# First mixer of a two-layer decoder step: all tokens per channel tile, 512-column convolution, weight matrices built on VectorE

## The reference

```python
def _conv_mixer(h, ctx, w_pw1, b_pw1, w_dw, b_dw, ln_g, ln_b, w_pw2, b_pw2):
    a = h @ w_pw1 + b_pw1                                        # (B, L, 2D)
    glu = a[..., :D_MODEL] * jax.nn.sigmoid(a[..., D_MODEL:])    # (B, L, D)
    full = jnp.concatenate([ctx.astype(glu.dtype), glu], axis=1) # (B, CONV_WIDTH-1+L, D)
    conv = lax.conv_general_dilated(
        full, w_dw[:, None, :].astype(full.dtype), window_strides=(1,), padding='VALID',
        dimension_numbers=('NWC', 'WIO', 'NWC'), feature_group_count=D_MODEL) + b_dw
    y = jax.nn.silu(_layernorm(conv, ln_g, ln_b))
    out = y @ w_pw2 + b_pw2
    return out, full[:, -(CONV_WIDTH - 1):]
...
        xp = xp + op
        xp = xp + _swiglu(_rmsnorm(xp, ffn_norm_g[i]), ffn_w_gate[i], ffn_w_up[i], ffn_w_down[i])
```

## Time and profile before

| | |
|---|---|
| three runs | 1807.9, 1812.1, 1810.9 us, median 1810.9 |
| profiled execution | 1810.1 us; span of its slowest core 1808.6 us |
| busy share of the span | TensorE 84%, VectorE 53%, ScalarE 22%, GpSimd 14% |
| granted clock of TensorE, mean | 0.92 |
| DMA | 124 MB, mean 69 GB/s |
| chain that ended last | TensorE 72%, VectorE 13%, issue 6%, ScalarE 4%, DMA 3% |

### The profile page before, as it was taken

The page is one execution under the profiler, slowest core; times in us unless marked ns, Lnnn a source line. Parts: engine busy times, 40 slices in busy tenths (PEclk is TensorE's granted clock), DMA queues, the critical chain, the costliest instruction groups (busy, mean ns, idle before and its releaser), DMA issues.

```text
span 1808.6 us, 24861 instructions; the slowest of 8 cores (1792.4 to 1808.6 us)
## 1 busy us (share of the span) xinstructions
PE 1525.7 (84%) x8314; PEld 726.9 (40%) x8314; DVE 956.1 (53%) x1328; ACT 398.2 (22%) x612; POOL 261.6 (14%) x158
## 2 busy tenths in 40 slices
PE   3777836676988999999995897797999999999973
PEld 1344414433434444444441443344444444444431
DVE  3398747375464252534349656865634252515278
ACT  3143453362220101010111322222110101010111
POOL 3185407510000000000002011001000000000011
PEclk8798978897989999999996998898999999999986
DMA  8952253364202040312124642213422121212013
GB/s 171 172 153 56 51 117 93 80 126 110 41 7 48 1 71 9 62 28 32 24 47 93 139 141 93 89 52 77 68 37 47 24 47 24 47 24 48 1 47 145
DMA packets 132303, 124.11 MB, mean 69 GB/s; under 512 B 5748, under 2 KB 119668, under 8 KB 131128
## 3 DMA queue, kind: packets, MB, share of 16 engines
q0 software_dynamic: 50800, 48.60, 18.1%
q1 hardware_dynamic: 81384, 73.93, 14.0%
HBM read 140.83 MB, written 31.98 MB: 96 GB/s over the span
## 4 chain that ended last, share of the span: by engine, by line
PE 72%; DVE 13%; issue 6%; ACT 4%; DMA 3%; POOL 1%; SPq 0%; DVEq 0%; ACTq 0%; POOLq 0%
PE ps L180 68%; DVE RSTD L285 3%; DVE HT L487 3%; PE ps L570 2%; DVE XT L886 2%; ACT CONV L612 1%; DVE YF L1217 1%; DVE CONV L601 1%; ACT L283 1%; PE ps L557 1%; DVE VB L1120 1%; POOL W L437 1%; DVE HCV L664 1%; DMA XT<-xt 1%; ACT RSTD L283 1%
## 5 line engine op out<-in xcount | busy, mean ns | idle before, releaser
L180 PE MATMUL ps<-HT,RB 128*128 128x512 bf16 x3328 | 750.2, 386 | 40.8 <-ACT RSTD L283 15.6
L180 PEld LDWEIGHTS ps<-HT,RB 128*128 128x128 bf16 x3328 | 325.7, 99 | 436.6 <-issue 70.1
L180 PE MATMUL ps<-HID,RB 128*128 128x512 bf16 (+1 forms) x1600 | 306.5, 352 | 37.8 <-DVE RSTD L285 22.7
L886 DVE TENSOR_TENSOR XT<-ps,XT 128x512 f32<-128x512 f32 (+1 forms) x480 | 270.8, 593 | 53.5 <-DVE XT L886 33.3
L180 PEld LDWEIGHTS ps<-HID,RB 128*128 128x128 bf16 x1600 | 139.0, 100 | 204.6 <-issue 65.2
L878 DVE TENSOR_TENSOR HID<-ps,SG 128x512 bf16<-128x512 f32 (+1 forms) x110 | 64.4, 597 | 250.4 <-PE ps L180 246.5
L878 DVE TENSOR_TENSOR HID<-ps,SGB 128x512 bf16<-128x512 f32 (+1 forms) x110 | 63.8, 596 | 243.9 <-PE ps L180 243.2
L180 PE MATMUL ps<-HT,RA 128*128 128x512 bf16 x752 | 175.1, 394 | 11.8 <-DVE CONV L601 11.7
L437 POOL TENSOR_TENSOR W<-IDS,WV 128x1152 bf16<-128x1152 bf16 x64 | 151.2, 2394 | 72.0 <-PE ps L570 63.4
L877 ACT ACTIVATE SGB<-ps 128x512 f32<-128x512 f32 (+1 forms) x110 | 57.4, 522 | 387.6 <-PE ps L180 386.8
L877 ACT ACTIVATE SG<-ps 128x512 f32<-128x512 f32 (+1 forms) x110 | 57.5, 522 | 380.9 <-PE ps L180 380.3
(11 more groups left out here) (126 smaller groups left out, 972.2 us busy)
## 6 DMA issues: line engine op xcount, KB each, us to landing
RB<-wsc_in SPq DMA_DIRECT2D x12, 1024.0 KB, 5.9
RB<-w_gate POOLq DMA_DIRECT2D x10, 1024.0 KB, 8.3
RB<-w_up POOLq DMA_DIRECT2D x10, 1024.0 KB, 9.9
RB<-w_down POOLq DMA_DIRECT2D x9, 1024.0 KB, 14.0
y_p<-YF SPq DMA_DIRECT2D x8, 1024.0 KB
RA<-w_pw POOLq DMA_DIRECT2D x12, 512.0 KB, 10.0
wsc_pw<-RA SPq DMA_DIRECT2D x12, 512.0 KB, 10.1
XT<-xt SPq DMA_DIRECT2D x6, 1024.0 KB, 12.5
```

What stands on the lines that cost most here:

```text
L180: fns.append(lambda o=o, l=l, r=r, i=i: nc.tensor.matmul(o, l, r, start=(i == 0), stop=(i == n - 1)))
L886: op(DVE, lambda: nc.vector.tensor_tensor(out=XT[:, m, t0:t0 + n], in0=ob[:, :n], in1=XT[:, m, t0:t0 + n], op=ALU.add), (obr,), (XTr[m][t],))
```

## The change

- x, HT and CONV are cut by token tile (`XTT`, `HTT`). Each channel tile is now projected for all 2048 tokens and the sample rows at once (`pw1_ct`), and convolved with 512 columns per matmul (`conv_ct`); there are no halves, no halo copies and no copy of the first mixer's weights in DRAM. Those are packed by the host so that a channel tile's block is contiguous.
- Each W9 is built once, 32 in all, by VectorE, five buffers. GpSimd only issues DMAs.
- The start goes token tile by token tile for the first three channel tiles. To make room, the W9 and CC buffers lie where x of token tile 2 was and GA and PR where tile 3 was, once these have been normalised. Tiles 2 and 3 of x are therefore read a second time ahead of the residual.
- Two PSUM banks hold the statistics, six rotate.
- The norm over channels comes after the last convolution, for tile 0, tile 1, then tiles 2 and 3 together. `y_move` takes half a token tile out and back, in pieces of 128 instead of 256 elements. `pw2` of tile 0 is cut in two: four input channel tiles for six outputs, then the other four.
- FFN0 begins with its 256-wide slice, woven into `pw2`, and ends with a whole one.

Its core, with lines left out:

```diff
...
-FFN0 = [(512 * s, 512) for s in range(5)] + [(2560, 256)]
+FFN0 = [(2560, 256)] + [(512 * s, 512) for s in range(5)]
...
-            i = (pstate["i"] % 8) if pstate["all"] else (1 + pstate["i"] % 7)
+            i = (pstate["i"] % 8) if pstate["all"] else (2 + pstate["i"] % 6)
...
+        W9 = [xat(f"W9_{i}", [128, NSH, 128], BF16, 32768 + 2304 * i) for i in range(NW9)]
+        CC = [xat(f"CC{i}", [128, 2, 512], BF16, 32768 + 11520 + 2048 * i) for i in range(2)]
+        GA = [xat(f"GA{i}", [128, 4, 8 + 512], BF16, 49152 + 4160 * i) for i in range(3)]
...
+        def load_w(c):
+            slot_load(RA[c % 3], w_pw1.rearrange("p (h b) n -> p h b n", h=2)[:, :, c, :])
+            return RA[c % 3].ap[:, :].rearrange("p (h k n) -> p h k n", h=2, k=8), RA[c % 3].res
...
-                op(POOL, lambda out=out, i0=i0, i1=i1: nc.gpsimd.tensor_tensor(out=out, in0=i0, in1=i1, op=ALU.mult),
-                   (IDSr, WVr), (W9r[sl],))
-
...
+        def w9_build():
...
+            w9["built"] += 1
+            sl = g % NW9
+            out = W9[sl][:].rearrange("p s (q i) -> p (s q) i", q=NPH)
+            i0 = IDS[:].unsqueeze(1).broadcast_to([128, NSH * NPH, 32])
+            i1 = WV[:, g, :].unsqueeze(2).broadcast_to([128, NSH * NPH, 32])
+            op(DVE, lambda: nc.vector.tensor_tensor(out=out, in0=i0, in1=i1, op=ALU.mult), (IDSr, WVr), (W9r[sl],))
...
+        def conv_group(g):
+            c, b = g // 4, g % 4
+            cv, cvr = bank()
+            sl = g % NW9
+            pe_multi([lambda s=s: nc.tensor.matmul(cv[:, :], W9[sl][:, s, :], GA[c % 3][:, b, 8 - s:520 - s],
+                                                   start=(s == 0), stop=(s == NSH - 1)) for s in range(NSH)],
+                     [GAr[c % 3], GAHr, W9r[sl]], (cvr,))
             conv_stats()
-            cs = CONV[:, 4 * c + 1:4 * c + 5, :]
-            op(DVE, lambda: nc.vector.tensor_copy(out=CC[:, :, 0, :], in_=cs), (CONVr[c],), (CBr,))
-            op(ACT, lambda: nc.scalar.activation(out=CC[:, :, 1, :], in_=cs, func=AF.Square),
-               (CONVr[c],), (CSQr,))
-            st_pend.append(c)
+            wr = [CONVr[t][c] for t in range(4)]
+            op(ACT, lambda: nc.scalar.activation(out=CONV[:, :, g + 1, :], in_=cv[:].rearrange("p (t u) -> p t u", t=4),
+                                                 func=AF.Identity, bias=vcol(V_PBDW, g), scale=1.0), (cvr, VECr), wr)
+            op(ACT, lambda: nc.scalar.activation(out=CC[g % 2][:, 1, :], in_=cv[:], func=AF.Square,
+                                                 bias=vcol(V_PBDW, g), scale=1.0), (cvr, VECr), (CCr[g % 2],))
+            op(DVE, lambda: nc.vector.tensor_copy(out=CC[g % 2][:, 0, :].rearrange("p (t u) -> p t u", t=4),
+                                                  in_=CONV[:, :, g + 1, :]), wr, (CCr[g % 2],))
+            st_pend.append(g)
+            w9_build()
...
+        def conv_ct(c):
+            for b in range(4):
+                conv_group(4 * c + b)
+                run(1)
...
+        def ln_act(t0, t1, k):
+            for g in range(8 * k, 8 * k + 8):
+                c = g // 4
+                wr = [CONVr[t][c] for t in range(t0, t1)]
+                if g % 4 == 0:
+                    wr += [CONVr[t][c - 1] if c else Y0r[t] for t in range(t0, t1)]
+                op(ACT, lambda g=g: nc.scalar.activation(out=YB[:, t0:t1, g, 0:128], in_=CONV[:, t0:t1, g + 1, :], func=AF.Silu,
                                                          bias=vcol(V_PLNB, g), scale=vcol(V_PLNG, g)), (VECr,), wr)
...
+        def y_move(t, hf):
+            d = ysc[2 * t + hf]
+            dr = Res()
+            rd = CONVr[t][4 * hf:4 * hf + 4] + [CONVr[t][3] if hf else Y0r[t]]
+            dma(SP, d.rearrange("p (g u) -> p g u", g=16), YB[:, t, 16 * hf:16 * hf + 16, 0:128], rd, (dr,))
             v = d.rearrange("(q j) (c b u) -> b j c q u", q=NPH, c=4, b=4)
-            dma_batch(SP, [(HTH[0][32 * b:32 * b + 32, c0:c0 + 4, :].rearrange("p c (q u) -> p c q u", q=NPH), v[b])
-                           for b in range(4)], (ymr[(h, c0)],), YR[h][c0:c0 + 4])
...
+        def pw1_ct(c):
+            for t in range(4):
+                pw1_unit(c, t)
+                run(1)
+            shuffle_out(c)
+            pw1_unit(c, 4)
+            if c + 3 < 8:
+                Wc[c + 3] = load_w(c + 3)
+            jobs.extend([lambda hf=hf: hist_job(c, hf) for hf in range(2)])
+
+        for c in range(3, 8):
+            pw1_ct(c)
...
+            conv_ct(c - 3)
+            shuffle_in(c)
+        jobs.extend([lambda: samp_new(6), lambda: samp_new(7), samp_fin, samp_ln])
+        conv_ct(5)
+        conv_ct(6)
+        run(len(jobs))
+        conv_ct(7)
+        conv_stats()
+        fM = fence([GSTr[2]])
+        for i in range(2):
...
+        conv_fin(0, 0, 128)
+        for k in range(4):
+            ln_dve(0, k)
+            ln_act(0, 1, k)
+            if k % 2 == 1:
+                y_move(0, k // 2)
+        for m in range(8):
+            pw2_unit(m, 4)
+        conv_fin(1, 128, 512)
+        for k in range(4):
+            ln_dve(1, k)
+            ln_act(1, 2, k)
+            if k % 2 == 1:
+                y_move(1, k // 2)
+        for c in range(8):
+            XTr[c][2] = Res(fence(W9r + CCr))
+            XTr[c][3] = Res(fence(GAr + [GAHr, PRr]))
+        xload(2, 1)
...
+        fC = [fence(CONVr[t] + [Y0r[t]]) for t in range(4)]
+        rb_open(0, fC[0])
+        rb_open(1, fC[0])
+        issue(2)
...
+        for m in range(6):
+            wP, rP = Pw[m // 2]
+            mc = (m % 2) * 128
+            pe_multi([lambda k=k: nc.tensor.matmul(banks0[m][0][:, :], wP[:, k, mc:mc + 128], pw2_mov(0, k),
+                                                   start=(k == 0), stop=False) for k in range(4)],
+                     YR[0][0:4] + [rP], (banks0[m][1],))
...
+                                                   start=False, stop=(k == 7)) for k in range(4, 8)],
+                     YR[0] + [rP], (banks0[m][1],))
+            pw2_res(banks0[m][0], banks0[m][1], m, 0)
+        for m in range(6, 8):
+            pw2_unit(m, 0)
+        for k in range(2):
+            for t in (2, 3):
+                ln_dve(t, k)
+            ln_act(2, 4, k)
+        y_move(2, 0)
+        y_move(3, 0)
+        norm_s1(0)
         for m in range(8):
...
+            pw2_unit(m, 1)
+        norm_s1(4)
+        for k in range(2, 4):
+            for t in (2, 3):
+                ln_dve(t, k)
+            ln_act(2, 4, k)
+        y_move(2, 1)
+        y_move(3, 1)
+        xload(3, 1)
+        fC = [fence(CONVr[t] + [Y0r[t]]) for t in range(4)]
+        rb_open(2, fence([Res(fC[0]), Res(fC[1])]))
+        rb_open(3, fC[1])
+        HID0 = at("HID0", [128, 4, TT], BF16, 33792)
+        HID0r = [[Res(fC[2]) for _ in range(NT)] for _ in range(4)]
+        f0n = FFN0[0][1] // 128
+        bg0, rg0 = next_block()
...
+        gu0 = lambda j, t: gate_up(bg0, rg0, bu0, ru0, HID0, HID0r, j, t)
+        norm_s2(0, V_FNG0)
+        norm_s1(1)
+        for j in range(f0n):
+            gu0(j, 0)
+        norm_s2(4, V_FNG0)
+        norm_rstd(1)
         for m in range(8):
-            pw2_unit(Pw[m // 2], RA[m // 2].res, m, 1)
...
+            pw2_unit(m, 2)
+            norm_app(1, V_FNG0, [m])
+        norm_s1(2)
+        for j in range(f0n):
+            gu0(j, 1)
+        norm_rstd(2)
         for m in range(8):
-            pw2_unit(Pw[m // 2], RA[m // 2].res, m, 4)
...
```

643 lines of the change are left out of this document (243 added, 400 removed).

## The result

The changed kernel takes 1833.6 us in its profiled execution (span 1832.5), against 1810.1 (span 1808.6) before; the ratio of the two kernels is 1.0129, 95% interval 1.0106 to 1.0152. I had forecast 1769.5 us and gave "slower" 8%. On the chip that ran n1_combo, n2_combo_ffn, n3_combo_pair and n4_noexch most executions, of the kernel before too, had one die (four cores) slowed, so those four runs stand without a ratio and are read by their rows and by the cores that were not slowed.

The account below looks back on a forecast made before the run. TensorE's waits and low clock in the first mixer were the target. Of 1808.6 us of span, 571.4 became 500 (119, 290, then 210 more), the wide slice added 30: 1767.2, plus 2.3 gives 1769.5 us; range 1745 to 1797.

Parts of the forecast that it names:

- Stage one: Start of the first mixer: three channel tiles projected for all tokens, x tile by x tile, ending at 119 us.
- tile 3's chain, to 100.6: Start of the first mixer: the norm chain of x tile 3 lets its matmuls start at 100.6 us.
- Stage two: Five projections (72.5 us), eight convolutions (76.4) and waits for VectorE (21.8), the last convolution matmul ending at 290 us.
- The statistics of a group wait for its cast: Convolutions: casts queue behind W and PR on VectorE; a group with a history job costs 4.05 us against TensorE's 2.38.
- the sixth 0.7: Sixth convolution: waits for VectorE add 0.7 us to its 9.5 us.
- In the seventh the norm of the sample rows: Seventh convolution: the sample's norm enters ScalarE's queue ahead of evictions, with casts behind it on VectorE, adding 8 us.
- Stage three: From the last convolution matmul to the first whole slice: norm, row exchange and VectorE's rounds, 210 us, ending at 500 us.
- 0.45 each: Convolution's norm after the last convolution: each Silu piece of 128 columns on ScalarE takes 0.45 us, eight 3.6 us.
- landing 4.6: Row exchange through DRAM: a y_move's rows land in 4.6 us at best, 6.6 in the middle.
- Rounds: End of the first mixer: gates (7 us), ONESM, root, RECIPROCAL and eight residual and HT pairs alternate through VectorE, to 210.
- Two: Rival, 18%: the row exchange is slow, each y_move in line costing 4.6 us more, 23 in all, giving 1793 us.
- three: Rival, 8%: slower than before, the exchange queue pacing the mixer's end as one serial chain, 49 us more, giving 1819 us.

Follow-up runs that it names:

- n1_combo: The changed kernel with the edits of m1_marks, m2_jobs, m3_quiet, m4_slot16 and q3_own_slot together; no ratio, six cores had 1762 to 1773 us.
- n2_combo_ffn: n1_combo with the first feed-forward slices ordered as before the change, 512 columns first and 256 last; medians of its dies 1779.9 and 1782.7 against 1769.8 us.
- n3_combo_pair: n1_combo with x tiles 0 and 1 normalised together, in Silus of 256 columns; the same kernel timed again had ratio 0.9803 to the kernel before.
- n4_noexch: The changed kernel without the exchange of rows through DRAM, so part of the computation is missing; 32 us earlier at the first whole slice, one execution.
- m4_slot16: The changed kernel, with the Silu of group 16 waiting only for its own slot, not the transfer out of groups 0 to 15; ratio 1.0081 to before.
- r2_before_signals: The kernel before the change, with every operation of ScalarE, VectorE and TensorE raising its semaphore; ratio 0.9763 to the kernel before.
- m1_marks: The changed kernel, with every operation of ScalarE, VectorE and TensorE signalling up to the first whole slice; ratio 1.0033 to the kernel before.
- q3_own_slot: The changed kernel, with a convolution's eviction no longer waiting for VectorE's cast of the group before; ratio 1.0082 to the kernel before.
- p4_w_gpsimd: The changed kernel with the 32 builds of W on GpSimd, as before the change; 1846.3 us in the one execution taken.
- m3_quiet: The changed kernel with x's second reads last in the exchange's queue and the first feed-forward weights after tile 1's rows; ratio 1.0118 to the kernel before.
- m2_jobs: The changed kernel with the history products, and four new-token sums, moved from the convolutions under the projections; ratio 1.0009 to the kernel before.

## Why the prediction was wrong

**What bounds the kernel: half right.** The slices and rates held (TensorE 345 of 347 us, 0.217 us per matmul, PR 1.15, and W 1.351, the value I took). By the Trainium skill ("Vector Engine (DVE) Microarchitecture Reference", Performance modes) two 16-bit elements go at once only where every operand's innermost step is 1 or -1; the trace agrees, with 1152 elements in 1351 ns where one operand has step 0. But I read waits by their sizes and took their releasers for needs. The earlier trace rows held one that wasn't: that for the transfer out of CONV (m4_slot16). The halo copy's in the earlier trace rows was a real need: with every operation signalling TensorE still waits for it. PE's waits in the kernel before, then in r2_before_signals (us in total, times, longest):

```profile
PE ps L570 <- ACT GA L707: 40.0, 4, 24.1
```
```profile
PE ps L572 <- ACT GA L709: 48.6, 4, 31.0
```

**Stage one, 11.4 us.** Failed step: "tile 3's chain, to 100.6", that is a unit paced by HT from the first HT on. It waited for the last of eight, and tile 2's for a GST (85.3 us). m1_marks moved these to 101.7 and 78.8 and the end to 134.3, against my 100.6, 80 and 133.5. The durations and the chain were right; that a wait ends when its operation does was assumed.

**Stage two, 20.5 us.** Failed step: "The statistics of a group wait for its cast". They waited for PR or a sum behind it, as ScalarE's evictions did. With signals alone (m1_marks) the stage takes 165.2 us instead of 177.0, so 11.8 of the 20.5 are late signals. A convolution is then 12.5 us where I had 12.0, and the first 13.4 where I had 12.6: the waits for VectorE's work, "the next four, with two each, 2.5 more", were nearly right (3.0; I had left out the sums of the new tokens, 1.36 us each, which also stand in that queue). In the changed kernel the same convolutions took 14.7 to 14.9. q3_own_slot (3 us) shows that the eviction's loop alone was not it, p4_w_gpsimd that W was better off on VectorE. Second failed step: "the sixth 0.7" and "In the seventh the norm of the sample rows" at 8. The sixth took 7.4 us more than 9.5 and the seventh 9.0, together 7.8 more than I gave them, and still 7.4 more in m1_marks. The queue of jobs reached the sample's norm at the end of the sixth (2.72 us of wait for VectorE's CB, 1.17 for its statistics), and VectorE's sums of the new tokens stood ahead of it. No run was made for this term alone. The projections, at 14.3 instead of 14.5, give about 1 back.

**Stage three, 34 us,** in three terms. *Silus*, 11 us: "0.45 each" was drawn between 64 columns (0.35) and 256 (0.67); a 128-column one takes 0.58 (9.29 for 16), 64 of them 8 us more, with a table load and the wait after it. *Landings*, 10 us ahead of tile 1: "landing 4.6" was taken from moves with nothing beside them, and I wrote that "DMA has little else there", though the change itself puts x's reads there and the first weights are free to start. m3_quiet has them at 5.7. *Rounds*, 12 us: from tile 0's HT (455.4) to the slice 110.5 us against 98; the gates run at 9.14 and 8.52 us instead of 7.0 after each wait, and the end waits 4.83 us for VectorE. That last wait is a late signal too: SCR at L960 is a clearing for layer 1, which the slice does not need, and in m1_marks it falls to 0.46 us, but there TensorE waits 5.54 us for w_up one block later. The rest of this term stays open; no run was made for it alone.

**The wide last slice** was right (30, measured 29.4), and so was the transfer out (4.5, measured 4.2). A move in 256-byte pieces therefore took 0.79 of the time of one in 512-byte pieces with twice the bytes. The Trainium skill ("DMA: Bandwidth & Descriptors", Specifications) says that below 512 bytes the engines read, modify and write. Read as I read it, as the whole cost for half the bytes (1.0), it was nearer to 0.79 than my lower end of 0.5, and it did not decide the case.

**Rivals.** Two and three named the exchange, at 23 to 49 us beyond my sum; the rows put its landings at 10 beyond it, and by n4_noexch all of the exchange is some 31. None named signals or ScalarE's Silus. The measured 1833.6 lies 14 us above even the slowest rival. The 8% for "slower" rested on one mechanism, where several ordinary ones added up: late signals 23 us in stages one and two, rounds 12, Silus 11, landings 10, the sample's norm 8. Each pushed the same way. And late signals are not why the changed kernel lost to the one before, which paid as much for them; they are why its own time was forecast too short, since my sum took the measured 571.4 us away, with its late signals, and put ideal waits in its place.

## What to carry to other kernels

Before you redesign a stage, look at who *releases* each wait and whether the waiter needs it; where the named operation is a later one on that engine, let the needed one signal first (43 us here from two added lines, without any redesign). Look where a queue of small jobs really puts each of them: moved under a stretch in which their engine is idle, they cost nothing (m2_jobs). When a transfer is moved or taken out of a cover, list everything that the same change lets start beside it.

## What the runs showed of the hardware

- VectorE, ScalarE and TensorE raising a semaphore with every operation (TensorE with the last matmul of a group) cost nothing that can be seen: four whole slices take 345.8 us in r2_before_signals, 347.8 without.
- The pace of short ScalarE work may depend on whether each waits for the one before. In the changed kernel the 128-column Silus of CONV, which do, last 493 ns and follow every 580; the 64-column ones of the sample, which don't, last 426 ns and follow every 345:

```profile
L597 ACT ACTIVATE CONV<-CONV,VEC 128x128 bf16<-128x128 f32 x64 | 31.5, 493 | 14.4 <-DMA ysc<-CONV 8.7
L671 ACT ACTIVATE HT<-HCV,VEC 128x64 bf16<-128x64 f32 x8 | 2.8, 426 | 0.0
```

  That would be why a value drawn between 64 and 256 columns was too low; no run took the waits away, so the cause is argued, not shown.
- Beside GpSimd's builds (p4_w_gpsimd) VectorE's plain cast slows too: from 427 to 880 ns on the mean, PR from 1150 to 1706.
